# Attention scores as six fp32r products of split operands in place of two fp32 products, in a hybrid DeltaNet and attention layer

## What is computed

```python
def block(args):
    i, q_i = args
    start = i * ATTN_BLOCK
    k_i = lax.dynamic_slice_in_dim(kp, start, band, axis=1)
    v_i = lax.dynamic_slice_in_dim(vp, start, band, axis=1)
    ...
    ok = (jnp.abs(qpos[:, None] - kpos[None, :]) <= WINDOW) & (kpos[None, :] >= 0) & (kpos[None, :] < length)
    s_win = jnp.einsum('bqkgd,bskd->bkgqs', q_i, k_i).astype(jnp.float32) * scale
    s_win = jnp.where(ok, s_win, -jnp.inf)
    s_ctx = jnp.einsum('bqkgd,bskd->bkgqs', q_i, k_ctx).astype(jnp.float32) * scale
    p = jax.nn.softmax(jnp.concatenate([s_win, s_ctx, sink_l], axis=-1), axis=-1).astype(v.dtype)
    return (jnp.einsum('bkgqs,bskd->bqkgd', p[..., :band], v_i)
            + jnp.einsum('bkgqs,bskd->bqkgd', p[..., band:band + n_ctx], v_ctx))
```

## Time and profile before

| | |
|---|---|
| median of 3 runs | 2553.68 us |
| profiled execution, its own time | 2558.28 us |
| its span in the trace | 2556.5 us |
| mean granted TensorE clock | 0.994 |
| PE busy in the span | 2455.8 us, 96% |
| PE weight loads | 2043.4 us, 80% |
| DVE | 1442.0 us, 56% |
| ACT | 808.5 us, 32% |
| POOL | 843.7 us, 33% |

### The profile page before, as it was taken

How to read it: one execution, slowest core, us unless ns; L and a number is a source line. 1 busy time by engine, 2 the same in 40 slices (tenths; PEclk the granted TensorE clock), 3 DMA queues, 4 the chain that set the end, 5 groups by cost and what they waited for, 6 DMA issues and landing times. The chain is left out here.

```text
span 2556.5 us, 40046 instructions
## 1 busy us (share of the span) xinstructions
PE 2455.8 (96%) x16022; PEld 2043.4 (80%) x16022; DVE 1442.0 (56%) x2274; ACT 808.5 (32%) x1833; POOL 843.7 (33%) x572
## 2 busy tenths in 40 slices
PE   5999999999999999999999989999899999999999
PEld 4668887888888888888888877878688888887887
DVE  6784665221666666666666663356855555555332
ACT  4222544110354554645555453101211111111100
POOL 1442753232424142322414132335433333332121
PEclk9999999999999999999999999999999999999999
DMA  7331331322100010100101012324411111113442
GB/s 271 80 80 53 116 125 60 115 74 83 34 18 27 17 34 9 43 26 18 34 10 34 1 43 91 99 88 129 148 50 50 50 50 50 50 37 124 124 135 90
DMA packets 52647, 177.00 MB, mean 69 GB/s; under 512 B 5360, under 2 KB 14960, under 8 KB 51184
## 3 DMA queue, kind: packets, MB, share of 16 engines
q1 hardware_dynamic: 50160, 170.24, 20.6%
q10 hardware_dynamic: 2304, 4.20, 0.4%
HBM read 148.20 MB, written 20.97 MB: 66 GB/s over the span
## 5 line engine op out<-in xcount | busy, mean ns | idle before, releaser
L205 PE MATMUL late_ps<-h_hi,late_w_hi 128*128 128x512 f32 x784 | 307.6, 392 | 6.1 <-ACTq L127 3.4
L206 PE MATMUL late_ps<-h_lo,late_w_hi 128*128 128x512 f32 x784 | 306.7, 391 | 0.0
L207 PE MATMUL late_ps<-h_hi,late_w_lo 128*128 128x512 f32 x784 | 306.5, 391 | 0.0
L188 POOL CAST late_w_hi<-late_w_raw 128x1024 fp32r<-128x1024 f32 x76 | 80.0, 1052 | 505.4 <-issue 378.0
L1415 PE MATMUL late_ps<-h_hi,dn_w_hi 128*128 128x512 f32 (+1 forms) x640 | 246.6, 385 | 0.0
L1415 PE MATMUL late_ps<-h_hi,dn_w_lo 128*128 128x512 f32 (+1 forms) x640 | 245.8, 384 | 0.0
L1415 PE MATMUL late_ps<-h_lo,dn_w_hi 128*128 128x512 f32 (+1 forms) x640 | 244.9, 383 | 0.0
L195 POOL TENSOR_TENSOR late_w_lo<-late_w_raw,late_w_hi 128x1024 fp32r<-128x1024 f32 x76 | 205.3, 2702 | 6.1
L2532 DVE SCALAR_TENSOR_TENSOR ffn_u<-ffn_pad,vectors,ffn_u 128x1024 f32<-128x1024 f32 (+1 forms) x90 | 198.1, 2201 | 3.2
L205 PEld LDWEIGHTS late_ps<-h_hi,late_w_hi 128*128 128x128 f32 x784 | 148.1, 189 | 37.6 <-issue 6.9
L206 PEld LDWEIGHTS late_ps<-h_lo,late_w_hi 128*128 128x128 f32 x784 | 148.3, 189 | 31.3 <-issue 0.2
(11 more groups left out here) (376 smaller groups left out, 6171.7 us busy)
## 6 DMA issues: line engine op xcount, KB each, us to landing
late_w_raw<-in_w_up SPq DMA_DIRECT2D x44, 512.0 KB, 3.5
down_w_raw<-in_w_down SPq DMA_DIRECT2D x32, 704.0 KB, 4.3
late_w_ada<-in_w_ada SPq DMA_DIRECT2D x8, 2048.0 KB, 7.8
dn_w_raw<-in_w_dn SPq DMA_DIRECT2D x32, 512.0 KB, 3.8
w_ada<-in_w_ada SPq DMA_DIRECT2D x8, 1024.0 KB, 11.6
at_w_raw<-in_w_mg_at SPq DMA_DIRECT2D x16, 512.0 KB, 3.9
late_w_raw<-in_w_mg_dn SPq DMA_DIRECT2D x16, 512.0 KB, 3.7
late_w_raw<-in_w_out SPq DMA_DIRECT2D x16, 512.0 KB, 3.8
```

Of the source, the lines that this page charges most:

```text
L188: pool.tensor_copy(self.hi[j][:, :, :], self.raw[j][:, :, :]).then_inc(self.hi_made, 1)
L205: pe.matmul(out, self.hi[j][:, k, :], xh, start=(k == 0), stop=False)
L206: pe.matmul(out, self.hi[j][:, k, :], xl, start=False, stop=False)
L207: mm = pe.matmul(out, self.lo[j][:, k, :], xh, start=False, stop=(k == self.kt - 1))
```

## The change

Three things are added, and one is replaced.

1. `parts` places the new tiles: high parts of the two key heads, of the context keys and of two units' queries, in SBUF that the context's input has left free. The low parts are written over the operands themselves (`a.qk_lo` is `a.qk`, `a.k_ctx_lo` is `a.k_ctx`, seen as fp32r).
2. In the projections, ACT makes the high parts of the two key heads, of the context keys and of the first two units' queries, one behind each copy of a value chunk (chunks 0 to 4). DVE makes the low parts at the end of its list.
3. In the window stage, ACT makes the high part of q of unit s+2 between the exponential of unit s and its copy L889 (`query_high`), and DVE makes the low part between the maximum of unit s+1 and `scale(s-1)` (`query_low`), with one subtraction of 128 columns that reads the query and its high part from SBUF.
4. In `scores(u)` the products L818 and L820 give way to six fp32r products: three over the window's 256 or 384 columns and three over the 256 context columns. PE waits for the low part of unit u's query ahead of the masks.

```diff
+                    if c < KV_HEADS:
+                        out_ready.wait(act, HEADS + c + 1)
+                        act.activation(a.k_hi[:, c, :], a.qk[:, HEADS + c, :], ACT.Copy).then_inc(k_hi_made, 1)
+                    elif c == KV_HEADS:
+                        act.wait_ge(kc_made, 1)
+                        act.activation(a.k_ctx_hi[:, :], a.k_ctx[:, :], ACT.Copy).then_inc(kc_hi_made, 1)
+                    elif c < KV_HEADS + 3:
+                        act.activation(a.q_hi[:, c - KV_HEADS - 1, :], a.qk[:, 0, (c - KV_HEADS - 1) * P:(c - KV_HEADS) * P],
+                                       ACT.Copy).then_inc(q_hi_made, 1)
...
+                for g in range(KV_HEADS):
+                    dve.wait_ge(k_hi_made, g + 1)
+                    dve.tensor_tensor(a.qk_lo[:, HEADS + g, :], a.qk[:, HEADS + g, :], a.k_hi[:, g, :].bitcast(F32), ALU.subtract)
...
-                    ps, q = ps_s[u % 2], a.qk[:, h, b * P:(b + 1) * P]
+                    ps, q_hi, q_lo = ps_s[u % 2], a.q_hi[:, u % 2, :], a.qk_lo[:, h, b * P:(b + 1) * P]
+                    if u >= 2:
+                        pe.wait_ge(q_lo_made, u - 1)
...
-                    pe.matmul(ps[:, c0:W0], q, a.qk[:, HEADS + g, win[0] * P:(win[-1] + 1) * P],
-                              start=False, stop=True, skip_group_check=True)
-                    pe.matmul(ps[:, W0:W0 + CTX], q, a.k_ctx[:, g * CTX:(g + 1) * CTX],
-                              start=True, stop=True).then_inc(scored.sem, 1)
+                    k_hi, k_lo = (k[:, win[0] * P:(win[-1] + 1) * P] for k in (a.k_hi[:, g, :], a.qk_lo[:, HEADS + g, :]))
+                    kc_hi, kc_lo = (k[:, g * CTX:(g + 1) * CTX] for k in (a.k_ctx_hi, a.k_ctx_lo))
+                    here, there = ps[:, c0:W0], ps[:, W0:W0 + CTX]
+                    pe.matmul(here, q_hi, k_hi, start=False, stop=False, skip_group_check=True)
+                    pe.matmul(here, q_hi, k_lo, start=False, stop=False, skip_group_check=True)
+                    pe.matmul(there, q_hi, kc_hi, start=True, stop=False)
+                    pe.matmul(there, q_hi, kc_lo, start=False, stop=False)
+                    pe.matmul(there, q_lo, kc_hi, start=False, stop=True)
+                    pe.matmul(here, q_lo, k_hi, start=False, stop=True, skip_group_check=True).then_inc(scored.sem, 1)
...
+                def query_high(u):
+
+                    h, b = divmod(u, XCH)
+                    act.activation(a.q_hi[:, u % 2, :], a.qk[:, h, b * P:(b + 1) * P], ACT.Copy).then_inc(q_hi_made, 1)
...
                         probs(s)
+                        if s + 2 < UNITS:
+                            query_high(s + 2)
                         evacuate(s)
...
+                def query_low(u):
+
+                    h, b = divmod(u, XCH)
+                    dve.wait_ge(q_hi_made, u - 1)
+                    dve.tensor_tensor(a.qk_lo[:, h, b * P:(b + 1) * P], a.qk[:, h, b * P:(b + 1) * P],
+                                      a.q_hi[:, u % 2, :].bitcast(F32), ALU.subtract).then_inc(q_lo_made, 1)
...
                         maximum(s + 1)
+                    if 0 <= s and s + 2 < UNITS:
+                        query_low(s + 2)
                     if 0 <= s - 1 < UNITS:
                         scale(s - 1)
```

More of the change, by code:

```diff
@@ L542, in attention_projections @@
         ba_t = core.sb("b_and_a_channel_major", [32, TOK], ctx=st)
+        k_hi_made, kc_made, kc_hi_made = core.sem("k_hi_made"), core.sem("k_ctx_made"), core.sem("k_ctx_hi_made")
+        q_hi_made = core.sem("first_q_hi_made")
         ctx_scaled, ctx_hi, ctx_lo = core.sem("ctx_scaled"), core.sem("ctx_hi"), core.sem("ctx_lo")
-        assert nc.sbuf_base <= core.x_ctx_at
+        assert nc.sbuf_base <= a.parts_at
         ba_banks = [ps_main[1][0:32, 0:HALF], ps_main[1][0:32, HALF:2 * HALF], ps_main[0][0:32, HALF:HALF + CTX]]
@@ L731, in _ @@
                 raw_ready.wait(dve, NT + 1)
-                dve.tensor_tensor(a.k_ctx[:, :], raw[:, 0:n], rs[:, 0:n], ALU.mult)
+                dve.tensor_tensor(a.k_ctx[:, :], raw[:, 0:n], rs[:, 0:n], ALU.mult).then_inc(kc_made, 1)
+                for g in range(KV_HEADS):
+                    dve.wait_ge(k_hi_made, g + 1)
+                    dve.tensor_tensor(a.qk_lo[:, HEADS + g, :], a.qk[:, HEADS + g, :], a.k_hi[:, g, :].bitcast(F32), ALU.subtract)
+                dve.wait_ge(kc_hi_made, 1)
+                dve.tensor_tensor(a.k_ctx_lo[:, :], a.k_ctx[:, :], a.k_ctx_hi[:, :].bitcast(F32), ALU.subtract)
+                for b in range(2):
+                    dve.wait_ge(q_hi_made, b + 1)
+                    dve.tensor_tensor(a.qk_lo[:, 0, b * P:(b + 1) * P], a.qk[:, 0, b * P:(b + 1) * P],
+                                      a.q_hi[:, b, :].bitcast(F32), ALU.subtract)
 def window_attention(core, d, a):
@@ L750, in window_attention @@
         ada_acc = core.sb("late_ada_sums", [P, 2, SLOT_T * P], ctx=st)
-        assert nc.sbuf_base <= ring_at(core)
+        assert nc.sbuf_base <= a.parts_at
         at_w = core.at_w
+        q_hi_made, q_lo_made = core.sem("q_hi_made"), core.sem("q_lo_made")
         ada_in, mod_made = core.sem("late_ada_in"), core.sem("late_mod_made")
@@ L1076, with parts @@
     pass
+def parts(core, a):
+    place = lambda name, shape, at: core.nc.alloc_sbuf_tensor_at(name, shape, F32R, offset=at)
+    a.parts_at = core.x_ctx_at - KV_HEADS * CTX * 4
+    a.k_ctx_hi = place("k_ctx_hi", [P, KV_HEADS * CTX], a.parts_at)
+    a.k_hi = place("k_heads_hi", [P, KV_HEADS, SEQ], core.x_ctx_at)
+    a.q_hi = place("q_unit_hi", [P, 2, P], core.x_ctx_at + KV_HEADS * SEQ * 4)
+    assert core.x_ctx_at + KV_HEADS * SEQ * 4 + 2 * P * 4 <= ring_at(core)
+    a.qk_lo = place("qk_heads_lo", [P, HEADS + KV_HEADS, SEQ], a.qk_at)
+    a.k_ctx_lo = place("k_ctx_lo", [P, KV_HEADS * CTX], a.k_ctx_at)
 def attention(core, d):
@@ L1082, in attention @@
         a.qk_norm = core.vec[:, V_QKN:V_QKN + HEADS + KV_HEADS]
+        a.qk_at = core.nc.sbuf_base
         a.qk = core.sb("qk_heads", [P, HEADS + KV_HEADS, SEQ], ctx=st)
+        a.k_ctx_at = core.nc.sbuf_base
         a.k_ctx = core.sb("k_ctx", [P, KV_HEADS * CTX], ctx=st)
         a.v_tok = core.sb("v_tok", [P, NCH, KV_HEADS * P], ctx=st)
+        parts(core, a)
         attention_projections(core, d, a)
```

## The result

The changed kernel takes 2574.32 us (median of four runs, 2567.74 to 2576.53); the kernel before, run beside it, 2554.02 (2553.59 to 2560.98). The ratio is 1.0066, with an interval of 1.0052 to 1.0081: the change makes the kernel slower. The medians are 20.3 us apart, the means 17.6. The profiled execution is the fastest of the four, 2567.74 us with a span of 2565.8. Only one stage of the program differs, so from here on I quote its length as well: the time from the transposes of the first unit to those of the last, read off PE's timeline. It was 196.9 us before and is 215.1 us now, 18.2 more.

The account below looks back on a forecast made before the run. It took PE's scores to be tied with ACT's and DVE's rounds, so shorter scores gain nothing in steady units. Terms -0.2 + 17.5 + 0.8 + 3 = +21 us put the median at 2553.7 + 21.1 = 2574.8 us, range 2561 to 2592.

Parts of the forecast that it names:

- The three-way tie, gain 0: Window stage, ahead of the transposes: PE's scores are tied with ACT's and DVE's rounds, so shorter products gain 0.
- The scores, 1.17 to 0.90 us: PE's products per three-block unit: 1.17 us removed, 0.90 added; the 0.27 saved all becomes idle time ahead of the transposes.
- The parts of k, the semaphores, `query_high`: ACT's and DVE's added copies and subtractions, six semaphores, and a 0.28 us ACT copy per unit: all hidden, cost 0.
- `query_low` is held until 0.1 us before POOL's end: DVE's two-SBUF-input subtraction stands until some 0.1 us before POOL's running instruction ends; rival, not held long: 2553.5 us, chance 0.10.
- Eight folds x 2.2 = 17.5 us: POOL's eight 4.52 us folds each hold a `query_low`, losing 0.6 to 3.8, mean 2.2 us; between 5 and 30 together.
- eight rounds of 5 to 7 us: Sign in the changed trace: eight window-stage rounds of 5 to 7 us in place of 3.19, the others still 3.19.
- Where the idle time stands: Sign: in the eight long rounds PE idles ahead of transposes L829, with DVE as releaser; each stall 2 to 3 us.
- L786 and the splits at 0 and 0.8: POOL's 0.69 us instructions hold `query_low` within its slack, cost 0; two 2.36 us weight splits cost 0.8 us together.
- The rival that runs the eight as one: POOL's eight L786 give DVE no turn between them: 24 us more, 2599 us; chance 0.05.
- The clock, half of the stalls, 0.85 each: After half of the eight stalls PE's clock drops, costing 0.85 us each: between 0 and 7, taken as 3 us.
- that rival: The clock falls for the whole stage since PE pauses more: 108 us more, 2662 us; chance 0.02.
- The sum: Whole kernel: -0.2 for the first unit's scores + 17.5 folds + 0.8 splits + 3 clock = +21 us.

Follow-up runs that it names:

- the second experiment: The changed kernel with each POOL fold cut into pieces of 256 columns, nothing left out: 2558.43 us, ratio 1.0009 to the kernel before.
- the tie taken apart: The kernel before, with ACT sending `result` one unit later, ahead of `evacuate`, and DVE copying ahead of `scale`: 2543.04 us, ratio 0.9950.
- the pair that differs in one input: The kernel before plus a spare 128-column DVE subtraction inside `maximum`, second input in PSUM or SBUF: 2556.95 us with PSUM, 2572.02 with SBUF.
- the new order: The changed kernel, folds whole, with ACT's `result` one unit later, ahead of `evacuate`, and DVE's copy ahead of `scale`: 2570.64 us, ratio 1.0053.
- the run with pieces: The changed kernel with ACT's `result` later, DVE's copy ahead of `scale`, and POOL's folds in pieces of 256 columns: 2544.03 us, ratio 0.9955.

## Why the prediction was right

It said 2574.8 us (2561 to 2592) and 0.86 for slower; measured were 2574.32 us and slower. The mechanism held, but that the number came within 0.5 us is luck: the folds, the splits and the clock were all put too high (17.5, 0.8 and 3 us against 15.2, 0 and 2.2), the stage grew by 18.2 us and not by 21, and the medians of two sets of four runs lie 20.3 apart where their means lie 17.6 apart.

- *The three-way tie, gain 0:* right. Undisturbed rounds stay at 3.18, and without the low part the stage is 197.0 against 196.9. With the tie taken apart the stage shrank from 196.9 to 184.1 us with the old scores: it was the order that held the round.
- *The scores, 1.17 to 0.90 us:* they take 0.96, from L844 at 282.68 to L849 at 283.46 and its own 0.18. The 384-column products start 0.17 to 0.18 us apart, as taken between 0.12 and 0.35, but the first one 0.26. All of it is idle time ahead of L857, 0.34 us where I said 0.4.
- *The parts of k, the semaphores, `query_high`:* 0, right. The five subtractions behind the projections took 3.7 us (some 4 expected) and no value chunk was late; `query_high` takes 0.30 us, and the second experiment shows all of it together in a stage of 197.4.
- *`query_low` is held until 0.1 us before POOL's end:* right, and now shown by the pair that differs in one input. Each long one ends 0.15 us after POOL's instruction; its own 0.28 us taken off, it starts 0.13 before. The Trainium skill, page "SBUF — State Buffer", section "Who interferes with whom", has a DVE instruction with two SBUF inputs and a GpSimd instruction that reads SBUF as blocking each other fully rather than sharing: by that rule, the traces agree (3.17 us with both inputs in SBUF, 0.28 with one in PSUM). Whether it is POOL's reads or its writes that hold DVE, no run here tells apart.
- *Eight folds x 2.2 = 17.5 us:* the count is right, the size was 1.9 each against the same rounds of before, 15.2. The holds were 2.62 us on average beyond the instruction's own 0.28 (I had the equivalent of 2.8), which is a matter of when the folds happen to start. The slack that follows is 0.7 on average, near the 0.64 taken, but between 0.25 and 1.0 from round to round, where I took one number for all. I had also followed DVE's own round only. PE waits for the low part directly: the masks L836 stand behind it, and the next transposes follow 256.15 - 254.93 = 1.22 us after `query_low`, against 283.98 - 281.93 = 2.05 in a free round, which gives 0.83. DVE's copy L963 is done at 255.98, just ahead of the last product (255.94 and its 0.18), so the two paths end almost together. And I had named eight rounds of 5 to 7 us as the sign, though my own 0.6 to 3.8 a fold gives 3.8 to 7; they lasted 3.90 to 6.56, six of them under 5.
- *Where the idle time stands:* wrong. I said ahead of the transposes with DVE as releaser; it is ahead of the masks of the next scores, 14.7 us in 8 waits. The releaser is DVE.
- *L786 and the splits at 0 and 0.8:* no `query_low` beside the 0.70 us instructions passed the slack, and none lasted longer than one POOL instruction; one split held it for 1.02 us, which cost no round above 3.6. The rival that runs the eight as one falls. The shorter folds were not all missed: 1.27 us ones were met twice, each time right behind the longest holds.
- *The clock, half of the stalls, 0.85 each:* two of eight, both behind the two longest holds, 4.48 and 4.23 us. The rounds behind them cost 1.55 and 0.69 us more than the same rounds before: 2.2 together, where I had 3. A `query_low` was held behind a short fold in each, so not all of it is the clock's. The clock did not fall for the stage (0.98 over the 196 us), so that rival falls.
- *The sum:* 15.2 + 2.2 leaves under 1 us of the stage's 18.2, spread over the 53 other rounds.

That the two profiled spans differ by 9.3 us only is no contradiction. The trace of before has 23.8 us at the 1.2 GHz level between 671 and 1822 us, where PE sets the pace, the trace of after 10.2. Two of these stretches, before and after:

```profile
1562.30:1569.10 6.80, 5.76 (x14) 4.54 (x15) 0.81 (x1) 4.96 (x5) 3.41 (x2) 0.51 0.79 286
```

```profile
1843.30:1850.10 6.80, 6.33 (x14) 3.73 (x14) 6.53 (x10) 3.53 (x5) 0.00 (x0) 0.50 0.47 189
```

13.6 us less at half the clock are up to 6.8 us of time that has nothing to do with the change. It may also be part of why the 29 runs of the kernel before that stood beside the first experiments scatter from 2547.5 to 2564.7 us: the mean granted clock was 0.996 in the fastest and 0.991 in the slowest, but between them time and clock go together only loosely. So a difference of spans is weaker evidence here than the length of the stage.

## What to carry to other kernels

Before you give DVE an instruction with two SBUF inputs, look for the longest GpSimd (POOL) instruction of that stretch: it can be held for nearly that long, so compare its length with the slack and not the instruction's own 0.28 us. Where such a meeting can't be avoided, cut GpSimd's instruction into short pieces; pieces of 0.73 us gave back the whole loss here. Another way may be an input in PSUM: the spare subtraction with one was not held, though the changed kernel was not run so. And before you shorten one engine's work, check whether others end at the same moment: shorter products were worth nothing until the order on ACT and DVE was changed, and that order alone was worth 12 us (2554.87 to 2543.04).

## What the runs showed that I had not expected

- A stage with less slack loses more to the same holds. With the new order, where PE has next to no idle time outside the holds, PE waited 24.5 us in 9 waits for a low part and the clock fell six times within the stage; with the old order 14.7 us in 8, and it fell twice. By stages the whole folds cost 22.1 us (209.2 against 187.1 with pieces) and 17.7 (215.1 against 197.4), and the 22.1 is too low, since the run with pieces has the waits for the sums, which the run with whole folds has not. The slack that hides a hold is the same slack that one removes. Whether the falls follow from the length of the pauses or from what surrounds them these runs don't tell apart: PE's longest wait for a low part was 3.9 us there and 3.5 us here.
- Halving the instruction that holds does not halve the loss: 18.2 us over before with 4.53 us folds, 13.2 with 2.35 us ones, of which some 1.5 stand in the two rounds at the first weight split. With pieces of 0.73 us it is gone; nothing between 0.73 and 2.35 was run.
- The hold goes the other way too. In the changed kernel three `query_low` began within 0.01 us of a fold of 512 columns, at 302.89, 326.93 and 353.25 us. They kept their 0.28 us, and the folds took 1.43 us in place of 1.27.
- DVE takes its turn between GpSimd instructions that stand ready back to back. Over 96 pieces of 0.73 us no `query_low` took more than 0.84 us.
- The version without the low part has a stage as long as before's (197.0 and 196.9 us), yet has a ratio of 1.0011 (1.0003 to 1.0020) over eleven runs. I have no row for this 0.1%.
